# Expert stage: down products of a unit issued behind the gate and up products of the next unit

## The reference, cut to what matters

```
def swiglu(x, wg, wu, wd):
    return (jax.nn.silu(x @ wg) * (x @ wu)) @ wd
...
routed = routed_experts(hf, idx, wts.astype(h.dtype), w_gate, w_up, w_down)
shared = swiglu(hf, sw_gate, sw_up, sw_down)
return (routed + shared).reshape(B, T, D)
```

## Time and profile before

| what | value |
|---|---|
| median of 3 runs | 2731.78 us (2728.42 to 2736.42) |
| the profiled execution's own time | 2731.99 us |
| its span | 2730.3 us |
| PE busy over the span | 2566.0 us (94%) |
| DVE, ACT, POOL busy | 1064.6, 671.0, 601.1 us |
| mean granted clock of TensorE | 0.977 of full speed |
| bytes read from and written to HBM | 396.20 and 27.71 MB |
| gate and up matmuls of the stage (L1633) | 1024, from 2099.75 us on |
| last down matmuls (L1649) begin | 2672.67 us |

### The profile page before, as it was taken

The page is one execution under the profiler, slowest core; times in us unless marked ns, Lnnn a source line. Parts: engine busy times, 40 slices in busy tenths (PEclk is TensorE's granted clock), DMA queues, the critical chain, the costliest instruction groups (busy, mean ns, idle before and its releaser), DMA issues. The chain is left out here.

```text
span 2730.3 us, 30805 instructions
## 1 busy us (share of the span) xinstructions
PE 2566.0 (94%) x10853; PEld 1553.7 (57%) x10853; DVE 1064.6 (39%) x2302; ACT 671.0 (25%) x1318; POOL 601.1 (22%) x539
## 2 busy tenths in 40 slices
PE   8998999899999999999999999999999999999991
PEld 7546888444666478874455447656755444444430
DVE  1125887103333266650033335556534223322215
ACT  2223444201333221210035532122122111111111
POOL 3017887210000144421121001101110111111110
PEclk9999999999999999999999999999989999999996
DMA  4234655631211233323232110100034899999985
GB/s 134 77 93 139 176 162 166 126 83 46 63 55 55 62 93 92 89 76 85 64 80 85 34 51 11 26 31 16 24 152 175 326 421 405 390 411 406 395 333 221
DMA packets 290661, 404.56 MB, mean 148 GB/s; under 512 B 14418, under 2 KB 253736, under 8 KB 264432
## 3 DMA queue, kind: packets, MB, share of 16 engines
q1 hardware_dynamic: 273808, 366.24, 38.9%
q0 software_dynamic: 15632, 34.44, 3.9%
q10 hardware_dynamic: 1104, 2.31, 0.2%
HBM read 396.20 MB, written 27.71 MB: 155 GB/s over the span
## 5 line engine op out<-in xcount | busy, mean ns | idle before, releaser
L900 PE MATMUL bank<-bring 128*128 128x512 f32 x704 | 305.2, 596 | 7.8 <-DMA bring<-f_w_down 7.8
L900 PEld LDWEIGHTS bank<-bring 128*128 128x128 f32 x704 | 134.7, 192 | 174.8 <-issue 166.3
L1633 PE MATMUL bank<-bring 128*64 128x512 f32 (+1 forms) x512 | 226.9, 596 | 0.8 <-ACT bring L2089 0.8
L961 PE MATMUL bank<-ysq 128*128 128x256 f32 x960 | 214.1, 380 | 0.0
L961 PEld LDWEIGHTS bank<-ysq 128*128 128x128 f32 x960 | 183.3, 191 | 24.5
L2159 DVE TENSOR_TENSOR xT<-bank,xT 128x512 f32<-128x512 f32 x32 | 22.1, 692 | 372.0 <-PE bank L900 371.9
L673 POOL TENSOR_TENSOR ysq<-ysq 128x512 f32<-128x512 f32 x23 | 29.2, 1269 | 592.1 <-ACT ysq L1713 526.8
L961 PE MATMUL bank<-hT,bring 128*128 128x256 f32 x640 | 144.8, 380 | 0.0
L682 POOL TENSOR_TENSOR two<-two 128x1024 f32<-128x1024 f32 (+2 forms) x72 | 122.2, 1698 | 67.8 <-ACT two L1733 46.4
L791 POOL TENSOR_TENSOR ffw<-two,maskT 128x512 f32<-128x512 f32 x40 | 52.2, 1313 | 383.9 <-DVE two L2548 316.5
L1633 PEld LDWEIGHTS bank<-bring 128*64 128x64 f32 (+1 forms) x512 | 78.1, 157 | 96.5 <-issue 96.5
(11 more groups left out here) (525 smaller groups left out, 4476.3 us busy)
## 6 DMA issues: line engine op xcount, KB each, us to landing
bring<-f_w_in SPq DMA_DIRECT2D x88, 512.0 KB, 5.2
bring<-exp_w_gate SPq DMA_DIRECT2D x32, 1024.0 KB, 11.3
bring<-exp_w_up SPq DMA_DIRECT2D x32, 1024.0 KB, 18.6
bring<-exp_w_down SPq DMA_DIRECT2D x32, 1024.0 KB, 20.5
two<-ada_w SPq DMA_DIRECT2D x24, 1024.0 KB, 5.3
bring<-f_w_down SPq DMA_DIRECT2D x16, 1408.0 KB, 7.1
two<-exp_w_gate SPq DMA_DIRECT2D x16, 1024.0 KB, 11.6
two<-exp_w_up SPq DMA_DIRECT2D x16, 1024.0 KB, 17.9
```

The source lines that it names most:

```text
L900: mm = pe.matmul(ps[BANKS[stage][n % 4]][:], w[:, k, n % per * P:(n % per + 1) * P], rhs[:, k, :], start=(k == 0), stop=(k == kb - 1))
L961: mm = pe.matmul(ps[bank][:, 256 * half:256 * half + 256], weights[:, k, :], rhs[:, k, :], start=(k == 0), stop=(k == 3))
L1633: mm = pe.matmul(ps[3][m * h:m * h + m, :].rearrange("p (m n) -> p m n", m=2), hgT[par][:, k, m * h:m * h + m], w, start=(k == 0), stop=(k ...
```

## The change

It moves work and loads in five places of the stage; no instruction is added or taken away.

- PE: `finish(u - 1)`, which is the down products of the unit before (and its shared step), now stands behind gate and up of u, both halves of the turned rows of u+1 and the slots of u+2, and ahead of turning the activations of u. The last unit's down products stand behind the loop.
- SP: the down load that follows G of a unit is now the one of the unit before (`waiting`), which waits for the down products of that unit.
- POOL: the scatter of a unit's results stands behind the gather that is issued one unit later.
- ACT: both halves of the turned rows are copied ahead of the copy of the turned activations.
- DVE: `take_y` and `shared_add` of u-1 stand behind the multiplications and slot rows of u.

```diff
@@ -556,13 +556,17 @@
             sp.wait_ge(s("rt_step"), 8)
             expert_in(3, bass.ds(3, 1), sems_of(3), DN)
 
+            waiting = ()
             for u, (first, n) in enumerate(UNITS):
                 chosen = [(q, bass.ds(sp.value_load(order_tab[0:1, q:q + 1], min_val=0, max_val=EXPERTS - 1), 1))
                           for q in range(first + 4, first + 4 + n) if q < EXPERTS]
-                for freed, count, parts in (("exp_gu", u + 1, GU), ("exp_down", 2 * u + 2, DN)):
-                    for q, e in chosen:
-                        sp.wait_ge(s(freed), count)
-                        expert_in(q % 4, e, sems_of(q), parts)
+                for q, e in chosen:
+                    sp.wait_ge(s("exp_gu"), u + 1)
+                    expert_in(q % 4, e, sems_of(q), GU)
+                for q, e in waiting:
+                    sp.wait_ge(s("exp_down"), 2 * u)
+                    expert_in(q % 4, e, sems_of(q), DN)
+                waiting = chosen
 
             def overflow_loads(q, n0):
                 begun = sp.to_reg(OV * (q + n0) + 1)
@@ -849,11 +853,16 @@
             pool.dma_start(fin_row, a["final_g_2"].partition_broadcast(P)).then_inc(s("g2_moved"), 16)
             pool.dma_start(g2_row, g2_dram.rearrange("b p -> (b p)").partition_broadcast(P)).then_inc(s("g2_moved"), 16)
 
+            def results_out(u):
+                pool.wait_ge(s("y_ready"), 2 * u + 2)
+                scatter(slot_row[:, u % 4:u % 4 + 1], yrow[u % 2]).then_inc(s(f"y{u % 2}_stored"), 16)
+
             for u in range(len(UNITS)):
                 if u + 2 < len(UNITS):
                     gather(u + 2)
-                pool.wait_ge(s("y_ready"), 2 * u + 2)
-                scatter(slot_row[:, u % 4:u % 4 + 1], yrow[u % 2]).then_inc(s(f"y{u % 2}_stored"), 16)
+                if u:
+                    results_out(u - 1)
+            results_out(len(UNITS) - 1)
 
             def overflow_rows(q, n0):
                 known, taken = pool.to_reg(OV * (q + n0) + 4), pool.to_reg(OV * (q + n0) + OV)
@@ -1651,34 +1660,39 @@
                                        start=(k == 0), stop=(k == 1))
                 return mm
 
+            def finish(u):
+                first, n = UNITS[u]
+                par, mine = u % 2, range(first, first + n)
+                pe.wait_ge(s("exp_actT"), u + 1)
+                for q in mine:
+                    pe.wait_ge(s(f"expdn{q % 4}_loaded"), 16 * (q // 4 + 1))
+                for half in range(2):
+
+                    wait(pe, s("y_ready"), 2 * u + half - 1)
+                    down(par, [q % 4 for q in mine], half).then_inc(s("exp_down"), 1)
+                if u in SHARED_UNITS:
+                    shared_down(u - SHARED_UNITS[0])
+
             for u, (first, n) in enumerate(UNITS):
                 par, mine = u % 2, range(first, first + n)
-                buffers = [q % 4 for q in mine]
                 for q in mine:
                     pe.wait_ge(s(f"expgu{q % 4}_loaded"), 32 * (q // 4 + 1))
                 pe.wait_ge(s("hgt_ready"), 2 * u + 2)
                 wait(pe, s("exp_act"), 2 * u)
-                gate_up(par, buffers).then_inc(s("exp_gu"), 1)
+                gate_up(par, [q % 4 for q in mine]).then_inc(s("exp_gu"), 1)
                 if u + 1 < len(UNITS):
-                    turn_rows(u + 1, 0)
+                    for half in range(2):
+                        turn_rows(u + 1, half)
                 if u + 2 < len(UNITS):
                     slots(u + 2)
+                if u:
+                    finish(u - 1)
                 wait(pe, s("exp_actT"), u)
                 for k in range(2):
                     pe.wait_ge(s("exp_act"), 2 * u + k + 1)
                     turned = turn_act_half(par, k)
                 turned.then_inc(s("exp_turned"), 1)
-                if u + 1 < len(UNITS):
-                    turn_rows(u + 1, 1)
-                pe.wait_ge(s("exp_actT"), u + 1)
-                for q in mine:
-                    pe.wait_ge(s(f"expdn{q % 4}_loaded"), 16 * (q // 4 + 1))
-                for half in range(2):
-
-                    wait(pe, s("y_ready"), 2 * u + half - 1)
-                    down(par, buffers, half).then_inc(s("exp_down"), 1)
-                if u in SHARED_UNITS:
-                    shared_down(u - SHARED_UNITS[0])
+            finish(len(UNITS) - 1)
 
             def overflow_expert(q, n0):
                 at = OV * (q + n0)
@@ -2103,12 +2117,11 @@
                 wait(act_e, s("exp_act"), 2 * u - 2)
                 nc.scalar.activation(esil[par], ps[3][:, 0:256], ACT.Silu).then_inc(s("exp_sil"), 1)
                 if u + 1 < len(UNITS):
-                    rows_turned(u + 1, 0)
+                    for half in range(2):
+                        rows_turned(u + 1, half)
                 act_e.wait_ge(s("exp_turned"), u + 1)
                 wait(act_e, s("exp_down"), 2 * u - 2)
                 nc.scalar.copy(eactT[par], ps[4][:, 0:256]).then_inc(s("exp_actT"), 1)
-                if u + 1 < len(UNITS):
-                    rows_turned(u + 1, 1)
 
             def overflow_expert(q, n0):
                 at = OV * (q + n0)
@@ -2766,6 +2779,16 @@
             dve.wait_ge(s("tokens_turned"), 4 * TT)
             dve.wait_ge(s("g2_moved"), 32)
             dve.wait_ge(s("tokens_taken"), 4 * TT + 1)
+            def results(u):
+                for half in range(2):
+                    dve.wait_ge(s("exp_down"), 2 * u + half + 1)
+                    if half == 0:
+
+                        wait(dve, s(f"y{u % 2}_stored"), 16 * (u // 2))
+                    take_y(u % 2, half).then_inc(s("y_ready"), 1)
+                if u in SHARED_UNITS:
+                    shared_add(u - SHARED_UNITS[0])
+
             for u in range(len(UNITS)):
                 par = u % 2
                 if u + 3 < len(UNITS):
@@ -2776,16 +2799,11 @@
                     act_half(par, k).then_inc(s("exp_act"), 1)
                 if u + 2 < len(UNITS):
                     slot_tokens(u + 2)
-                for half in range(2):
-                    dve.wait_ge(s("exp_down"), 2 * u + half + 1)
-                    if half == 0:
-
-                        wait(dve, s(f"y{par}_stored"), 16 * (u // 2))
-                    take_y(par, half).then_inc(s("y_ready"), 1)
+                if u:
+                    results(u - 1)
                 if u < 3:
                     weights_of((2 * u, 2 * u + 1))
-                if u in SHARED_UNITS:
-                    shared_add(u - SHARED_UNITS[0])
+            results(len(UNITS) - 1)
 
             left = Order(dve, s("ov_left"))
```

## The result

| | median | lowest to highest | runs |
|---|---|---|---|
| before | 2732.16 us | 2728.42 to 2736.42 | 7 |
| changed | 2742.15 us | 2736.56 to 2746.22 | 7 |

The ratio is 1.0029 with a 95% interval of 1.002 to 1.0039: the change made the kernel 10 us slower. The forecast was 2728.5 us with a range up to 2737 us, so the result lies outside it, and on the other side of before.

What follows compares the result with a forecast made beforehand. The prediction took one full DMA queue of weight loads to bound 505 us of the stage; -4.5 + 2.9 - 1.9, with two terms at 0, made -3.5 us on 2731.99, so 2728.5 us, range 2713 to 2737.

Steps and rivals of the forecast that it cites:

- (e): Other queues (SP, POOL, ACT, DVE): scatter keeps its distance from gate and up, the later gather stays hidden; 0 us.
- The gather's slack: On POOL, the gather issued 0.5 us later stays hidden, by 0.6 us in PE's pace and 1.7 in the queue's.
- PE's own unit: One unit at PE's own pace in the stage: 12.62 us before, 12.05 us with the DVE and ACT waits covered.
- (a): Start of the weight-load queue: G8 is issued sooner, since u0 has no down products ahead of u1; -4.5 us.
- (b): Load D7 leaves the time when the queue ran empty and joins its full part, 1 MB more; +2.9 us.
- (c): End of the stage: PE ends 12.3 us after the last landing instead of 14.2; -1.9 us.
- (d): Middle of the stage: same bytes through the same queue in another order, PE waiting 2.2 us a pair; 0 us.
- Room in the queue: Rival, chance 0.22: late in the stage a faster PE lifts the DMA rate from 393 to 422 GB/s; 2714 us.
- The thin queue: Rival, chance 0.14: buffers kept a unit longer leave fewer loads queued, late DMA share under 0.96; 2739 us.
- The cover is not there: Rival, chance 0.04: PE's wait moves to the gather or ACT's row copies, a unit stays 12.6 us; 2731.7 us.

Runs made afterwards that it cites:

- e1: The changed kernel with 8 columns instead of 4 for the slot rows and tokens: 2728.81 us, ratio to before 0.9983.
- e8: The kernel before with POOL's scatter moved behind the gather of the next unit, and 8 slot columns instead of 4: 2736.95 us, ratio 1.0009.

## Why the prediction was wrong

**The step that failed** is (e), in its sentence on POOL: "The scatter keeps its distance from gate and up." It does, but from gate and up of the *next* unit: from its own it moved a whole unit away. The term was put at 0 and cost 12.8 us, the stage of the changed kernel against that of e1 (584.9 and 572.1 us); their ratios to before, 1.0029 and 0.9983, are 12.6 us apart. I asked what stands behind the scatter on POOL and not who waits for its landing. The answer stood in the code, one line in `slot_tokens`, and it had a slack that could be worked out: the scatter's landing of 8.5 us or more behind gather and down, against a need 1.1 us behind gate and up of the next unit. With the scatter about 7 us behind gate and up, it lands near 15.5 and is needed near 13.2. It was late on paper by 2 us. In e1, where nothing waits for it, the trace bears this out: the scatter is issued some 6 us and lands 14.7 us behind gate and up. Once DVE is late, POOL issues the gather late and the scatter right behind it, such a scatter takes 11 us to land and not 8.5, and the loop of 13.3 us is closed.

**The wrong forecast in kind.** The prediction named the sign to look for: "I would be wrong in kind if PE waited in the stage for anything but weights." It did, by 39.5 us.

**The gather's slack** in (e), 0.6 us in PE's pace, was right by its own terms; once DVE's wait is taken away (e1), no wait for gathered rows is left at all.

**What PE gains.** Right: the 16.4 us and the 9.3 us of the earlier trace rows are gone in the changed kernel as in e1. PE's own unit was put at 12.05 us; in e1 two G issues a unit apart stand at 2600.86 and 2612.61, 11.75 us, and a pair takes 23.7 us early in the stage, so PE gained a little more.

**(a), (b), (c)**, tested by e1, where nothing else stands in front of them. Start of the queue: forecast 4.5 us sooner and at most 4.9, measured 57.0 - 51.4 = 5.6. D7: forecast 2.9 us more in the queue, measured (560.1 - 51.4) - (562.5 - 57.0) = 3.2, which holds (d) as well. End: forecast 12.3 us behind the last landing, measured 572.1 - 560.1 = 12.0. The sum was -3.5 and came out at 572.1 - 576.6 = -4.5; the medians of e1 and before differ by 4.6. That 505 us of the stage are one DMA queue, so that PE's 26 us of waits could not be won, was right.

**(d)**, put at 0, was right in e1 over the whole queue, though not in its detail. PE's waits for weights don't come as 2.2 us in each pair: there are 11, from u10 on, of up to 4.9 us, with pairs between them that run at PE's pace. In the changed kernel the loop decided instead: its queue took 11.3 us more than before, of which D7 was to be 2.9, and its end 2.9 us more where 1.9 less was forecast.

**The rivals.** *Room in the queue*: e1 is the test, and it falls. From G8's issue to the last landing (DMA view, first before, then e1):

```profile
DMA packets 35167, 199.16 MB, mean 394 GB/s; under 512 B 8121, under 2 KB 8121, under 8 KB 13632
```

```profile
DMA packets 35350, 200.15 MB, mean 393 GB/s; under 512 B 8190, under 2 KB 8190, under 8 KB 13687
```

One megabyte more at the same rate: PE's faster units turned into waits for weights. The sign named for this rival, a late pair of 25 us or less, would have misled. G58 and G61 stand 23.87 us apart in e1, but then G62 comes only 16.8 us behind G61; from u28 to u40 a pair takes 26.4 us in the mean, before 26.2. One pair is no measure of the queue when PE's waits come in lumps. The estimate from the Trainium skill ("DMA: Bandwidth & Descriptors", section "Where 436 GB/s comes from"), 20 us more by the ports' ceiling of 435 GB/s, did not come either; in no run here does a stretch of 40 us of the stage pass the 422 GB/s of the earlier trace rows. *The thin queue* named 2739 us and is the nearest number, but for the wrong reason. By its own sign it fails: the late share is 0.98, above its 0.96, no wait for a down weight is left, and e1, which keeps every load in the changed order, is fast. *The cover is not there* was right that the wait could "move to another place, the gather", but took the unit for 12.6 us and the cause for a missing cover. It had 0.04 and no price for a loop.

## What to carry to other kernels

When a step is moved by one stage of a pipeline, every buffer that it reads stays taken one stage longer, also the small ones: list for each operand who waits to write it next, and count the depth of its ring against the new distance. A buffer that a DMA reads comes free only at the DMA's landing, 8 to 11 us behind its issue here, and two in-order queues between two such landings make a loop whose period should be worked out and set beside the engine's. Where the queue of weight transfers is the limit, shorter waits on the compute engine are worth only what they do to the queue's first and last loads.

## What the runs showed of the hardware

A scatter's time to landing differs with what else is in flight. The last scatter, with the weights all landed, took 3.67 us in the chain of the changed kernel; in the stage the same instruction took 11.3 us in the changed kernel and 8.5 before (DMA issues from 2180 to 2260 us, first the changed kernel, then the one before, then e8; the last row is the chain's):

```profile
y_dram<-xT,slot_row POOLq DMA_INDIRECT x6, 11.3
```

```profile
y_dram<-xT,slot_row POOLq DMA_INDIRECT x6, 8.5
```

```profile
y_dram<-xT,slot_row POOLq DMA_INDIRECT x7, 11.2
```

```profile
2691.91 3.67 DMA y_dram<-xT,slot_row
```

The scatter that follows a gather by 1.4 us takes 2.8 us longer than one that follows it by 5 us. In e8, where no engine waits for a scatter and it follows the gather by 1.3 us, it takes 11.2 us; in e1, 4 us behind, 8.7. So the loop is not what makes it long; its place close behind a gather goes with it in every run. The trace lists both under one DMA queue; whether that is the cause no run here tried.
